# A decoder step's RWKV-7 state chain: the inverse folded into the reading matrix, and three engine orders rewritten

## The chip, the cores and the metric

The kernel runs on one core of a Trainium2 chip. The metric is the device time of one execution in microseconds (us).

## The reference

One step of a two-layer decoder over 512 prompt tokens and 8 sequences of 8 sampled tokens: a sliding-window attention layer, a SwiGLU layer, an RWKV-7 time mixing layer, and another SwiGLU layer, each with its normalisation. The change lies wholly in the RWKV-7 recurrence, for each of 16 heads of width 64:

```
sa = einsum('bhvk,bhk->bhv', S, -kk_t)
S  = S * d_t + sa * (kk_t * a_t) + v_t * k_t
o  = einsum('bhvk,bhk->bhv', S, r_t)
```

## The kernel before

**Stages.** Attention, the first SwiGLU layer and the projections r, k, v run until 868 us of the profile. The recurrence runs from there to 1248 us, the output projection and the second SwiGLU layer to the end. The time outside the recurrence is large products (line 779), which the change does not touch.

**The recurrence in chunks.** The 512 tokens are cut into 8 chunks of 64 (`NCH`, `CH`). Two heads, a pair, fill the 128 partitions. In a chunk the dependence of each token on the earlier ones is a triangular system. Its inverse `tt` is built without the state, and only then does the state `S_c` pass through the 8 chunks of the pair. For each chunk the state chain has four hops:

- TensorE `chain_u` (1178): u = (masked key-z product) v + z S_c, then VectorE `chain_u` (2458) copies it to `uc`;
- TensorE `chain_sa` (1193): tt times uc, then ScalarE `chain_sa` (1866) copies it to `sac`;
- TensorE `chain_s` (1204) adds b times sac to the state's bank, and VectorE `chain_s` (2463) scales it and writes `S_c`. ScalarE `scaled_state` (1861) prepares `spc` for that.

**Units and slots.** Unit 0 is the sampled tokens of all pairs, units 1 to 8 are the pairs of the prompt. The program is a software pipeline of 11 slots, s = 1 to 11, each with 8 steps c = 0 to 7. In slot s the engines prepare unit i = s (decays, keys; flag A1), build the inverse and the products of unit a = s-1 (A2), update the sampled state of pair j = s-2 (SB), run the state chain of pair q = s-3 (B), and normalise and gate pair g = s-4 (C). Slots 4 to 8 have all of it; slot 9 lacks A1, slot 10 has only B and C, slot 11 only C. Every engine has its own in-order list of this, written by hand (lines 1343 to 1424 for TensorE, 1931 to 2001 for ScalarE, 2543 to 2617 for VectorE). An engine that waits holds up all that stands behind in its list. ScalarE's `kk_root`, `gn_root`, `key_mix`, `merge_y`, `inverse_blocks`, VectorE's `masked_gram` and `hat`, and TensorE's `gram_*`, `level_*`, `merge_*`, `variance`, `bonus`, `gate` are such items. A `gram_` product goes to a bank of PSUM, and `masked_gram` reads it out.

**The transposed tokens.** The chain needs v, b and k of a unit with tokens on the partitions. VectorE transposes 32 by 32 blocks (`turned`, 2407) into a staging buffer, and SyncE moves the blocks to `tok` with 8 DMAs for each (`turned_in`, 548 to 554). There are two staging buffers: v and k share `reset`, b has `cc_s`. So k can't be transposed before v's copies have landed. In before that transpose stands at the end of step c = 2, ahead of the chain's copy of step 3.

**SyncE's queue in slot s** (569 to 582) is, in order: the 8 copies each of v, b and k; the store of a finished state `pw`; then a wait for the sampled state `sout`, which ScalarE writes as the last item of the slot; its store (580); and 8 loads of the sampled state of the slot after next (`state_in`, 541). The v copies of the next slot stand behind these. `sout` itself follows TensorE's `sample_update` (1265).

Of the kernel before, what the change touches and what calls it, by code (L numbers as in the profile page):

```python
# [22 lines left out]
P = 128  # L23
D = 1024
# [120 lines left out]
def build_program(nc, ins, outs, scratch):  # L145
    cols, width = constant_layout()
    ctx = ExitStack()
    with ctx:
# [14 lines left out]
        def const(name):  # L163
# [21 lines left out]
         tok_s, uc, sac) = region(  # L185
# [5 lines left out]
            ("gr", [P, 2, 3, SEQ], F32), ("tt", [P, 2, NCH, CH], F32), ("zr", [P, 3, NCH, 2, CH], F32), ("oS", [P, 2, SEQ], F32),  # L191
            ("g2h", [P, D], F32R), ("g2l", [P, D], F32R), ("g2m", [3 * G_REST, D], F32R), ("tok_s", [P, 3, SEQ], F32), ("uc", [P, 2, HD], F32),
# [83 lines left out]
        def tt_of(i):  # L276
            return tt[:, (i - 1) % 2] if i else tt_s
# [139 lines left out]
        def _(sp):  # L417
# [126 lines left out]
            def turned_in(i, which, name):  # L544

                sp.wait_ge(ev("turned_" + name), i + 1)
                if i >= 3:
# [214 lines left out]
        def _(pe):  # L762
# [284 lines left out]
            def lora2(i):  # L1047
# [4 lines left out]
                if i >= 2:  # L1052
                    pe.wait_ge(ev("kr"), i - 1)
                    pe.wait_ge(ev("kz"), i - 1)
                if i:
# [20 lines left out]
            def diag_gram(i):  # L1076
# [5 lines left out]
                if i >= 2:  # L1082
                    pe.wait_ge(ev("tt12"), i - 1)
# [61 lines left out]
            def gram_kz(i):  # L1145

                pe.wait_ge(ev("sig_a"), min(i + 2, UNITS))
                if i >= 3:
                    pe.wait_ge(ev("z"), i - 2)
                for c in range(NCH):  # L1150
                    for part in heads2:
                        out = mm(ps[part, G2, tk(c)], column(kx, i, part, c), zr_of(i)[part, c, 0, :], start=True, stop=True)
                out.then_inc(ev("kz_mm"), 1)

# [8 lines left out]
            def chain_ready(q):  # L1163

                for name in ("kz", "tt"):
                    pe.wait_ge(ev(name), q + 2)
                for name in ("tok_b", "tok_k", "tok_v"):
                    pe.wait_ge(ev(name), TURNED * (q + 2))
                pe.wait_ge(ev("tt12"), q + 1)
# [8 lines left out]
            def chain_u(q, c):  # L1178

                o = ps[:, CU, 0:HD]  # L1180
                if c == 0:
                    for part in heads2:
                        out = mm(o[part], gr[part, q % 2, 2, tk(0)], tok[part, q % 2, 2, tk(0)], start=True, stop=True)
                else:
                    pe.wait_ge(ev("sup"), NCH * q + c)
                    for part in heads2:
                        out = mm(o[part], zr[part, q % 3, c, 0, :], S_c[part, c - 1, :], start=False, stop=True)
                out.then_inc(ev("u"), 1)
# [101 lines left out]
            def variance(g):  # L1290
# [3 lines left out]
                pe.wait_ge(ev("kz"), min(g + 3, UNITS))  # L1294
# [36 lines left out]
            def gate_s(j):  # L1331

                at = slice(j * P, (j + 1) * P)
                mm(ps[:, IV, tk(j)], g2h[:, at], sgh[:, 0, SEQ:T], start=True, stop=False)
# [8 lines left out]
            def slot(s):  # L1343
# [9 lines left out]
                for c in range(NCH):  # L1353
                    if B:
                        chain_u(q, c)
# [7 lines left out]
                    elif c == 2 and C:  # L1363
                        centred(g)
                    elif c == 3:
                        if A2:
                            level_x(a, 2)
                        if CSM:
                            variance_s()
                    elif c == 4 and C:  # L1370
                        variance(g)
                    elif c == 5:
                        if whole:
                            level_y(a, 4)
                        if SB:
                            sample_read(j)
                        if CSM:
                            bonus_s()
                    elif c == 7 and whole:
                        merge_t(a)  # L1380
                    if B:
                        chain_sa(q, c)
                    if c == 2 and A2:
                        level_y(a, 2)
                    elif c == 4 and whole:
                        level_x(a, 3)
                    elif c == 5 and C:
                        bonus(g)
                    elif c == 6:
                        if SB:  # L1390
                            sample_sa(j)
                        if whole:
                            merge_y(a)
                        if C:
                            gate(g)
                    elif c == 7:
                        if A2:
                            gram_kz(a)
                        if SB:
                            sample_update(j)  # L1400
# [4 lines left out]
                    if c == 0 and A1:  # L1405
                        lora2(i)
                    elif c == 1 and A2:
                        level_x(a, 1)
                    elif c == 2 and A1:
                        kk_sum(i)  # L1410
                    elif c == 3 and whole:
                        level_y(a, 3)
                    elif c == 5:
                        if whole:
                            level_x(a, 4)
                        if SB:
                            sample_u(j)
                    elif c == 6:
                        if SB:
                            sample_out(j)  # L1420
                        if A2:
                            gram_br(a)
                    elif c == 7 and A2:
                        gram_kr(a)
# [21 lines left out]
        def _(act):  # L1446
# [419 lines left out]
            def chain_sa(q, c):  # L1866
# [4 lines left out]
                A(sac[:, c % 2, :], ps[:, CU, HD:P], ACT.Copy).then_inc(ev("sac"), 1)  # L1871
# [59 lines left out]
            for s in range(1, SLOTS):  # L1931
# [11 lines left out]
                for c in range(NCH):  # L1943
                    if B and c >= 1:
                        scaled_state(q, c)
                    if c == 0 and whole:
                        corner(a)
                    elif c == 1 and A2:
                        level_y(a, 1)
                    elif c == 2:  # L1950
                        if C:
                            dev_squares(g)
                        if CSM:
                            dev_squares_s()
                    elif c == 3 and A1:
                        kk_root(i)
                    elif c == 5 and whole:
                        level_y(a, 4)
                    elif c == 6:
                        if A1:  # L1960
                            key_mix(i)
                        if s == SLOTS - 1:
                            for b in range(2):
                                split_high(PH["ro"], b, b)
                    elif c == 7:
                        if whole:
                            merge_t(a)
                    if B:
                        chain_sa(q, c)
# [686 lines left out]
```

## Time and profile before

| | us |
|---|---|
| runs | 1768.16, 1763.10, 1766.89; median 1766.89 |
| profiled execution, its own time | 1760.71 |
| its span | 1758.9 |
| TensorE matmul busy | 1617.8 |
| VectorE busy | 889.4 |
| ScalarE busy | 629.3 |
| mean granted TensorE clock | 0.953 of full |

The span is the time from the first to the last instruction of the profiled execution. All times below count from the start of the span.

### The profile page before, as it was taken

The numbers are of one execution on the slowest core, as the hardware profiler recorded it, in microseconds if no ns is written. First come the engines' busy times: TensorE is split into PE (matmuls) and PEld (weight loads), VectorE is DVE, ScalarE is ACT, GpSimd is POOL, SyncE is SP. The second block draws the span as 40 slices with busy tenths as digits, with TensorE's granted clock in tenths as the row PEclk, the third lists the DMA queues.
The fourth block names the chain that finished last, engine by engine and source line by source line (L and its number), as shares of the span: only waits on it lengthen the run. The fifth ranks groups of instructions, "written<-read, shape, count | busy, mean of one in ns | idle before, by whom it ended". The sixth has DMA issues, their size and how long they took to land.

```text
span 1758.9 us, 44459 instructions
## 1 busy us (share of the span) xinstructions
PE 1617.8 (92%) x19218; PEld 1498.2 (85%) x19218; DVE 889.4 (51%) x1225; ACT 629.3 (36%) x1051; POOL 613.4 (35%) x322
## 2 busy tenths in 40 slices
PE   6989999999999977999878888888999999999995
PEld 6976999999999976888856666666799999999994
DVE  2156776666543237623354555543476666553233
ACT  3266333323221124333444455533343323322113
POOL 3335434434443321223332232310334444443430
PEclk9999999999999997999968999989799999999997
DMA  6610232222232223222222222210422222223221
GB/s 200 184 34 25 77 123 74 82 83 83 80 98 83 82 64 94 102 61 73 63 34 41 36 39 37 38 33 16 132 79 75 81 83 84 83 79 97 83 66 54
DMA packets 306018, 133.59 MB, mean 76 GB/s; under 512 B 119035, under 2 KB 302892, under 8 KB 305716
## 3 DMA queue, kind: packets, MB, share of 16 engines
q1 hardware_dynamic: 300850, 121.80, 25.7%
q10 hardware_dynamic: 5026, 9.70, 1.5%
q8 instruction: 112, 1.84, 0.4%
q14 instruction: 30, 0.25, 0.0%
HBM read 116.86 MB, written 12.64 MB: 74 GB/s over the span
## 4 chain that ended last, share of the span: by engine, by line
PE 77%; DVE 8%; issue 5%; SPq 5%; ACT 3%; DMA 1%; POOL 1%; ACTq 0%; DVEq 0%; POOLq 0%
PE ps L779 63%; SPq L554 3%; SPq L541 2%; DMA tok<-reset 1%; POOL wl L612 1%; ACT S L1654 1%; PE ps L1107 1%; PE ps L1197 1%; PE ps L1297 1%; PE ps L1027 1%; DVE xl_all L2070 1%; DVE mf L2327 1%; PE ps L1117 1%; PE ps L1302 1%; PE ps L1233 1%
## 5 line engine op out<-in xcount | busy, mean ns | idle before, releaser
L612 POOL TENSOR_TENSOR wl<-raw,wh 128x1024 fp32r<-128x1024 f32 (+1 forms) x172 | 479.8, 2790 | 780.1 <-ACT wh L1455 780.1
L779 PE MATMUL ps<-xh_all,wh 128*128 128x290 f32 (+1 forms) x2112 | 462.4, 300 | 29.0 <-DVE xl_all L2146 14.3
L779 PE MATMUL ps<-xh_all,wl 128*128 128x290 f32 (+1 forms) x2112 | 457.1, 298 | 0.0
L779 PE MATMUL ps<-xl_all,wh 128*128 128x290 f32 (+1 forms) x2112 | 456.3, 297 | 0.0
L1455 ACT CAST wh<-raw 128x1024 fp32r<-128x1024 f32 (+1 forms) x172 | 191.0, 1112 | 589.9 <-PE ps L779 581.5
L779 PEld LDWEIGHTS ps<-xh_all,wh 128*128 128x128 f32 x2112 | 344.0, 191 | 39.9 <-issue 15.9
L779 PEld LDWEIGHTS ps<-xl_all,wh 128*128 128x128 f32 x2112 | 343.3, 191 | 0.0
L779 PEld LDWEIGHTS ps<-xh_all,wl 128*128 128x128 f32 x2112 | 342.6, 191 | 0.0
L779 PE MATMUL ps<-hh,wh 128*128 128x288 f32 x704 | 148.1, 292 | 0.0
L779 PE MATMUL ps<-hl,wh 128*128 128x288 f32 x704 | 148.1, 292 | 0.0
L779 PE MATMUL ps<-hh,wl 128*128 128x288 f32 x704 | 148.1, 292 | 0.0
L2039 DVE TENSOR_TENSOR x<-x,ps 128x576 f32 (+1 forms) x32 | 24.1, 754 | 217.6 <-PE ps L779 211.1
L2183 DVE SCALAR_TENSOR_TENSOR lnw<-lnw,up_sc 128x576 f32<-128x576 f32 x44 | 122.2, 2777 | 1.5
L779 PEld LDWEIGHTS ps<-hh,wh 128*128 128x128 f32 x704 | 112.0, 187 | 0.0
L779 PEld LDWEIGHTS ps<-hl,wh 128*128 128x128 f32 x704 | 111.9, 187 | 0.0
L779 PEld LDWEIGHTS ps<-hh,wl 128*128 128x128 f32 x704 | 111.9, 187 | 0.0
L2048 DVE TENSOR_TENSOR lnw<-lnw 128x576 f32<-128x576 f32 x32 | 90.8, 2837 | 4.1 <-ACT lnw L1482 3.3
L2177 DVE COPY up_sc<-ps 128x2 f32<-128x2 f32 x44 | 7.0, 159 | 159.1 <-PE ps L779 159.1
L1575 ACT ACTIVATE hh<-lnw 128x576 fp32r<-128x576 f32 x44 | 30.1, 685 | 148.1 <-DVE lnw L2183 148.1
L706 POOL TENSOR_TENSOR zl<-oS,zh 128x512 fp32r<-128x512 f32 x8 | 10.1, 1268 | 172.0 <-ACT zh L1916 172.0
L2174 DVE SCALAR_TENSOR_TENSOR lnw<-lnr,gate_sc,lnw 128x576 f32<-128x576 f32 x44 | 58.5, 1329 | 4.7
L1573 ACT ACTIVATE lnw<-lnw,gate_sc 128x576 f32<-128x576 f32 x44 | 34.2, 777 | 69.3 <-DVE lnw L2174 69.3
(364 smaller groups left out, 2212.5 us busy)
## 6 DMA issues: line engine op xcount, KB each, us to landing
raw<-in_ffn_w_gu SPq DMA_DIRECT2D x88, 512.0 KB, 3.7
raw<-in_ffn_w_down SPq DMA_DIRECT2D x32, 704.0 KB, 4.4
raw<-in_rwkv_w_rkv SPq DMA_DIRECT2D x24, 512.0 KB, 3.7
raw<-in_attn_w_qkv SPq DMA_DIRECT2D x24, 256.0 KB, 3.5
raw<-in_attn_w_o SPq DMA_DIRECT2D x32, 128.0 KB, 2.9
tok<-reset SPq DMA_DIRECT2D x128, 32.0 KB, 2.4
raw<-in_rwkv_w_o SPq DMA_DIRECT2D x8, 512.0 KB, 3.7
spread<-table ACTq DMA_DIRECT2D x1, 3072.0 KB, 14.9
```

The costliest lines, as they stand in the source:

```text
L541: sp.dma_start(nat[block_rows(h, e), j % 2].rearrange("p b (f k) -> p b f k", f=2)[:, :, f], own[e][:, :, f]).then_inc(ev(f"nat_in{j % 2}" ...
L554: sp.dma_start(dst[block_rows(h, f), :, e], src[block_rows(h, e), :, f]).then_inc(ev("tok_" + name), 16)
L612: nc.gpsimd.tensor_tensor(wl[:, s, 0:ph.kb, :], raw[:, s, 0:ph.kb, :], wh[:, s, 0:ph.kb, :].bitcast(F32), ALU.subtract).then_inc(raw_free, 1)
L779: out = mm(ps[:, 2 * a + b, 0:n], w[:, s, k, :], o[:, k, b, 0:n] if wide else o[:, k0 + k, t0:t0 + TH], start=(first and k == 0 and w is w ...
L1027: out = mm(ps[part, bank + b, 0:TH], g1s[:, k, cols], mf[:, k % 2, t0:t0 + TH], start=(k == 0), stop=(k == KB - 1))
L1455: nc.scalar.copy(wh[:, s, 0:ph.kb, :], raw[:, s, 0:ph.kb, :]).then_inc(hi_done, 1)
L1573: A(gbuf[:, q, :], gbuf[:, q, :], ACT.Silu, bias=gate_sc[:, q, 1:2]).then_inc(ev("gated"), 1)
L1575: A(hh[:, bass.ds(2 * i + q, 1), :], hbuf[:, q:q + 1, :], ACT.Copy).then_inc(hid_hi, 1)
L2039: V.tensor_tensor(blk, blk, acc(a), ALU.add).then_inc(acc_free, 1)
L2048: V.tensor_tensor(squares, squares, lnw[:, 3:4, :], ALU.add).then_inc(ev("ln_acc"), 1)
L2174: V.scalar_tensor_tensor(g, centre, gate_sc[:, q, 0:1], g, ALU.mult, ALU.add).then_inc(ev("ffn_step"), 1)
L2183: V.scalar_tensor_tensor(h, h, up_sc[:, 1:2], g, ALU.add, ALU.mult).then_inc(up_free, 1)
```

## The change

The inverse is multiplied into the matrices that read the state, once for each unit, so that the chain loses the hop through `uc`: `chain_u` now yields sa itself. TensorE gets two new groups of 16 matmuls for each of units 1 to 8, `fold_read` (the masked product times the inverse) and `fold_seen` (z times the inverse). ScalarE copies each out of the bank (`folded_read`, `folded_seen`). For `fold_seen`, z is needed in transposed form as well, so VectorE has a fourth transpose, through the buffer `cc_s` that b uses, and SyncE 8 more copies, between b's and k's. `tt` has one buffer instead of two. The key-z product of units 1 to 8 is taken in the other orientation, and its mask is applied by one instruction with two operations.

The orders are rewritten. "Ahead" is between the chain's first and second product of a step, "behind" is after the second:

| step | TensorE ahead | TensorE behind | VectorE before its chain item | VectorE after it |
|---|---|---|---|---|
| 0 | diag_gram | lora2, centred | v transpose, sample_state | level_first |
| 1 | level_y 1 | level_x 1 | b transpose | level_x 1 |
| 2 | sample_read, level_y 2 | level_x 2 | cumulated | level_x 2 |
| 3 | kk_sum, level_y 3, sample_u | level_x 3 | sample_ut | kk_floor, level_x 3 |
| 4 | gram_kz, level_y 4, sample_sa | level_x 4 | sample_u, z transpose | level_x 4, unit_keys |
| 5 | variance, merge_y | merge_t | kz mask | k transpose, scaled_z |
| 6 | gram_br, bonus, sample_out | fold_read, gram_kr | hat, br mask | bonus, scaled_b |
| 7 | gate | fold_seen, sample_update | kr mask | sample_out, gated, mixed_keys, bonus_terms |

ScalarE's list has, after the chain's copy: step 3 level_y, kk_root, dev_squares; step 4 level_y, sample_sa, chunk_decays; step 5 merge_y, inverse_blocks, gn_root; step 6 folded_read, key_mix (and merge_t ahead of the chain's copy, behind scaled_state); step 7 folded_seen, operand_high, sample_update.

The diff, cut to what is not in the table:

```diff
-            return reset[:, PADP:PADP + SEQ] if which != 0 else cc_s[:, 0:SEQ]
+            return reset[:, PADP:PADP + SEQ] if which in (1, 2) else cc_s[:, 0:SEQ]
...
+        def turned_b_at(i):
+
+            return 2 * i if i else 1
+
+        def turned_z_at(i):
+
+            return 2 * i + 1
...
-                dst = tok_of(i)[:, which, :].rearrange("p (c e n) -> p c e n", e=2, n=HB)
+                dst = (ztok[:] if which == 3 else tok_of(i)[:, which, :]).rearrange("p (c e n) -> p c e n", e=2, n=HB)
...
-                    for which, name in ((2, "v"), (0, "b"), (1, "k")):
-                        turned_in(s - 1, which, name)
+                    turned_in(s - 1, 2, "v", s)
+                    turned_in(s - 1, 0, "b", turned_b_at(s - 1))
+                    if s >= 2:
+                        turned_in(s - 1, 3, "b", turned_z_at(s - 1))
+                    turned_in(s - 1, 1, "k", s)
...
+            def fold_read(i):
+
+                pe.wait_ge(ev("tt"), i + 1)
+                pe.wait_ge(ev("tt12"), i)
+                pe.wait_ge(ev("kz"), i + 1)
+                for c in range(NCH):
+                    for part in heads2:
+                        out = mm(ps[part, IV, tk(c)], gr_of(i)[part, 2, tk(c)], tt_of(i)[part, c, :], start=True, stop=True)
+                out.then_inc(ev("folded_mm"), 1)
+
+            def fold_seen(i):
+
+                pe.wait_ge(ev("folded"), read_at(i))
+                pe.wait_ge(ev("tok_b"), TURNED * turned_z_at(i))
+                for c in range(NCH):
+                    for part in heads2:
+                        out = mm(ps[part, IV, tk(c)], ztok[part, tk(c)], tt_of(i)[part, c, :], start=True, stop=True)
+                out.then_inc(ev("folded_mm"), 1)
...
-                out.then_inc(ev("u"), 1)
+                out.then_inc(ev("sa"), 1)
...
-            def chain_sa(q, c):
-
-                pe.wait_ge(ev("uc"), NCH * q + c + 1)
-                for part in heads2:
-                    out = mm(ps[part, CU, HD:P], tt[part, q % 2, c, :], uc[part, c % 2, :], start=True, stop=True)
-                out.then_inc(ev("sa"), 1)
...
-                pe.wait_ge(ev("kz"), min(g + 3, UNITS))
+                pe.wait_ge(ev("kz"), min(g + 4, UNITS))
...
+            def folded_read(i):
+
+                act.wait_ge(ev("folded_mm"), read_at(i))
+                A(gr_of(i)[:, 2, :], psb(IV), ACT.Copy, scale=-1.0).then_inc(ev("folded"), 1)
+
+            def folded_seen(i):
+
+                act.wait_ge(ev("folded_mm"), seen_at(i))
+                A(zr_of(i)[:, :, 0, :], chunks(psb(IV)), ACT.Copy).then_inc(ev("folded"), 1)
...
+                if which == 3:
+                    out, src = chunks(out), zr_of(i)[:, :, 0, :]
...
-            def chain_u(q, c):
-
-                dve.wait_ge(ev("u"), NCH * q + c + 1)
-                V.tensor_copy(uc[:, c % 2, :], ps[:, CU, 0:HD]).then_inc(ev("uc"), 1)
...
+                    elif c == 1 and A2:
+                        turned(a, 0, "b", "tok_b", 2 * a - 1 if a else 0)
...
+                        if whole:
+                            turned(a, 3, "b", "tok_b", turned_b_at(a))
...
+                        if A2:
+                            turned(a, 1, "k", "tok_v", a + 1)
```

## Rows read from the trace of the kernel before

**Rows 1.** Timeline of the SyncE queue: start, length, line, DMA, count.
```profile
885.00 5.59 SPq L554 DMA_DIRECT2D tok_s<-reset  x8
...
923.98 1.37 SPq L580 DMA_DIRECT2D out_sw<-sout  x2
...
963.91 1.33 SPq L580 DMA_DIRECT2D out_sw<-sout  x2
...
1045.01 1.31 SPq L580 DMA_DIRECT2D out_sw<-sout  x2
1046.37 5.64 SPq L541 DMA_DIRECT2D nat<-in_state_wkv  x8
...
1058.84 6.32 SPq L554 DMA_DIRECT2D tok<-cc_s  x8
1065.26 5.52 SPq L554 DMA_DIRECT2D tok<-reset  x8
...
1166.67 1.31 SPq L580 DMA_DIRECT2D out_sw<-sout  x2
...
1205.74 1.63 SPq L580 DMA_DIRECT2D out_sw<-sout  x2
```

**Rows 2.** Chain of waits in slots 5 and 6: start, length, who held it.
```profile
1024.53 1.99 PE ps L1297 x2
...
1031.37 1.07 PE ps L1302 x2
...
1038.39 0.96 PE ps L1142 x32
...
1041.63 0.86 PE ps L1274 x4
...
1043.35 0.95 PE ps L1279 x32
...
1058.13 3.74 DMA tok<-reset
```

**Rows 3.** The tile cc_s: its copies issued by SyncE, and their landing.
```profile
L554 SPq DMA_DIRECT2D tok<-cc_s x64: 585/611/1768, 899.9 to 1183.7; - x64
...
DMA to landing us min/median/max: 1.9/2.0/3.8
```

**Rows 4.** VectorE timeline of slot 6; in brackets the idle time before.
```profile
1061.89 0.71 DVE L2424 STREAM_TRANSPOSE reset<-kx 128x512 f32<-128x512 f32 x1 [3.69 <-DMA tok<-reset]
...
1069.98 0.74 DVE L2492 SCALAR_TENSOR_TENSOR oS<-ps,prm,rsd 128x512 f32<-128x512 f32 x1
...
1075.40 0.41 DVE L2449 TENSOR_TENSOR xt<-xt,ps 128x256 f32<-128x256 f32 x1
```

**Rows 5.** TensorE timeline of slot 6.
```profile
1062.76 0.48 PE L1197 MATMUL ps<-uc,tt 64*64 64x64 f32 x4 [4.00 <-DVE uc L2461]
...
1066.24 1.65 PE L1297 MATMUL ps<-rsd,cst 128*128 128x512 f32 x2
```

**Rows 6.** Costliest groups by line, over the whole span.
```profile
L1197 PE MATMUL ps<-uc,tt 64*64 64x64 f32 x256 | 22.6, 255 | 17.7 <-DVE uc L2461 16.9
...
L2461 DVE COPY uc<-ps 128x64 f32<-128x64 f32 x64 | 13.3, 208 | 8.8 <-PE ps L1187 8.7
```

**Rows 7.** ScalarE timeline of slot 6.
```profile
1069.03 0.63 ACT L1911 ACTIVATE rsd<-rsd 128x512 f32<-128x512 f32 x1
...
1077.69 0.76 ACT L1840 ACTIVATE yb<-ps 32x256 f32<-32x256 f32 x2 [0.40 <-PE ps L1125]
...
1082.34 1.68 ACT L1858 ACTIVATE tt<-xt 32x256 f32<-32x256 f32 x4
```

**Rows 8.** TensorE timeline of slot 10.
```profile
1206.27 0.28 PE L1183 MATMUL ps<-tok,gr 64*64 64x64 f32 x4
...
1235.81 0.48 PE L1175 MATMUL ps<-cst,S_c 64*64 64x64 f32 x4
```

**Rows 9.** VectorE timeline of slot 2: the v transpose.
```profile
892.46 0.67 DVE L2424 STREAM_TRANSPOSE reset<-vv 128x512 f32<-128x512 f32 x1
```

More of the change, by code:

```diff
@@ L1354, in slot @@
                     if B:
[L1355 removed]
+                        chain_sa(q, c)
                     if c == 0 and A2:
@@ L1362, in slot @@
                             centred_s()
-                    elif c == 2 and C:
-                        centred(g)
-                    elif c == 3:
-                        if A2:
-                            level_x(a, 2)
+                    elif c == 2:
+                        if SB:
+                            sample_read(j)
+                        if A2:
+                            level_y(a, 2)
+                    elif c == 3:
+                        if A1:
+                            kk_sum(i)
+                        if whole:
+                            level_y(a, 3)
+                        if SB:
+                            sample_u(j)
                         if CSM:
                             variance_s()
-                    elif c == 4 and C:
-                        variance(g)
-                    elif c == 5:
+                    elif c == 4:
+                        if A2:
+                            gram_kz(a)
                         if whole:
@@ L1375, in slot @@
                         if SB:
-                            sample_read(j)
+                            sample_sa(j)
+                    elif c == 5:
+                        if C:
+                            variance(g)
+                        if whole:
+                            merge_y(a)
                         if CSM:
                             bonus_s()
[L1379 to L1388, printed above, removed]
                     elif c == 6:
+                        if A2:
+                            gram_br(a)
+                        if C:
+                            bonus(g)
                         if SB:
[L1391 to L1400, printed above, removed]
+                            sample_out(j)
+                    elif c == 7 and C:
+                        gate(g)
                     if CSM:
@@ L1404, in slot @@
                         chain_s(q, c)
-                    if c == 0 and A1:
-                        lora2(i)
+                    if c == 0:
+                        if A1:
+                            lora2(i)
+                        if C:
+                            centred(g)
                     elif c == 1 and A2:
                         level_x(a, 1)
-                    elif c == 2 and A1:
-                        kk_sum(i)
+                    elif c == 2 and A2:
+                        level_x(a, 2)
                     elif c == 3 and whole:
-                        level_y(a, 3)
-                    elif c == 5:
-                        if whole:
-                            level_x(a, 4)
-                        if SB:
[L1417 to L1424, printed above, removed]
+                        level_x(a, 3)
+                    elif c == 4 and whole:
+                        level_x(a, 4)
+                    elif c == 5 and whole:
+                        merge_t(a)
+                    elif c == 6:
+                        if whole:
+                            fold_read(a)
+                        if A2:
+                            gram_kr(a)
+                    elif c == 7:
+                        if whole:
+                            fold_seen(a)
+                        if SB:
+                            sample_update(j)
             for s in range(1, SLOTS):
@@ L1945, in _ @@
                         scaled_state(q, c)
+                    if c == 6 and whole:
+                        merge_t(a)
+                    if c == 2 and CSM:
+                        dev_squares_s()
+                    if B:
+                        chain_sa(q, c)
                     if c == 0 and whole:
                         corner(a)
[L1948 to L1969, printed above, removed]
-                    if c == 1:
+                    elif c == 1:
+                        if A2:
+                            level_y(a, 1)
                         if A1:
@@ L2405, in bonus_terms, with turned @@
                 V.tensor_tensor(own, own, kx[:, :, SEQ:T], ALU.mult).then_inc(ev("f"), 1)
-            def turned(i, which, name, earlier, count):
+            def turned(i, which, name, free, count):
                 if count:
-                    dve.wait_ge(ev(earlier), TURNED * count)
+                    dve.wait_ge(ev(free), TURNED * count)
                 if which == 1:
```

186 lines of the change are left out of this document (109 added, 77 removed).

## The prediction

> **What bounds the kernel now.** Only the stage of the recurrence, 868 to 1248 us, changes, and in it the length of a slot is what counts. I took the SyncE queue's timeline first. The stores of the sampled state mark the slots: slot 3 ends at 963.91 and slot 8 at 1166.67 [rows 1], five slots of 40.55 us. Then I followed the chain of waits through one slot. In it the reader is to see a loop that runs through the queue. From the store of `sout` at 1045.01 SyncE issues two stores, eight loads (5.64 us from 1046.37), then the v copies, which end when b's begin at 1058.84 [rows 1]. The last v copy lands 3.74 us after its issue at 1058.13 [rows 2]. Only then can VectorE transpose k at 1061.89, after 3.69 us of idleness [rows 4]. The chain's next item stands behind it, so TensorE idles 4.00 us and comes back at the lower clock [rows 5]. From the store to the end of that transpose are 17.6 us; from there to the next `sout` some 23.6 us of steps 3 to 7.
>
> The hop that the change removes is on this path only in those steps. TensorE idle before the tt product and VectorE idle before the copy are 17.7 and 8.8 us in the whole stage [rows 6].
>
> **The parts of the change, and their cost.** I follow the same loop in the new order.
>
> *The hop.* 64 copies of 0.208 us go from VectorE, and 64 pairs of products with their wait from TensorE [rows 6]. On a bare chain a hop is 0.33 + 0.21 and the signals, some 0.6 us, 4.8 for each pair; in a full slot the long groups cover most.
>
> *The k transpose* goes from step 2 to step 5. In the rows v lands 16.9 us after the store (1061.87 less 1045.01) [rows 1, 2]; step 5 is later than that, so this wait is gone. What is late next is the z transpose in step 4. It uses `cc_s`, and must wait until b's copies of the same unit have landed. They are issued by 1058.84 + 6.32 = 1065.16, 20.15 us after the store [rows 1]. The last takes 0.61 and lands 2.0 after its start [rows 3], so at +21.5. With the transpose itself, about 0.7 like k's [rows 4], it ends at T = +22.3. When would VectorE have arrived? By adding up steps 0 to 3 in the table's order (diag_gram, lora2, centred and level 1 some 7 us, then steps of 3 to 3.7 us set by a level and the ScalarE work between) I get some 16 us after the slot's start. VectorE stands idle for about 6 us, longer than now.
>
> *Behind it* stand the chain item of step 4, level_x 4, unit_keys, and the kz mask, and TensorE's `variance` now waits for that mask. Times after T: chain item 0.3; level_x two instructions of 0.41 and about 0.45 [rows 4]; unit_keys 0.74, by the hat of the same shape and kind [rows 4]; mask 0.7. `variance` starts at 2.8, not at 1.2, and at the low clock takes 2.0 [rows 2], to 4.8. merge_y, the chain's second product, merge_t and the next first product take 2.9, to 7.7. ScalarE has merge_y's copies (0.76), inverse_blocks (1.68) and gn_root (0.68 + 0.63) one after another [rows 7], from 5.6 to 9.4. So `bonus` waits until 8.85 and ends at 9.9, and the second product of step 6, whose `sac` copy stands behind gn_root, scaled_state and merge_t's 0.76, starts at 10.85. After it fold_read and gram_kr, 0.96 each like gram_br [rows 2], to 13.4. Step 7: first product 0.55, gate 1.15, second product 0.6, fold_seen 0.96, sample_update 0.86 + 0.86 + 0.95 [rows 2], to 19.35. `sout` and its signals 0.65: 20.0.
>
> The loop is thus 22.3 + 20.0 = **42.3 us, against 40.55: 1.75 more in each of slots 4 to 8, +8.8.** Fewer hops in steps 5 to 7 don't show, because gram_br, gram_kr and the fold groups now stand there and in before some of the work of these steps lay in the wait's shadow.
>
> *The new copies of z* cost SyncE 8 x 0.61 and gaps, by b's row 6.3 [rows 1]. They end at T + 6.3 and land by T + 7.8, ahead of fold_seen at T + 15.7; k's end at T + 12.6 and land at T + 14.5, ahead of the next slot at T + 19.4. The queue, with `pw`, is free at T + 13.9, before `sout`. They cost nothing while that cover of 5 us stands; the floor they set is 22.3 + 13.9 = 36.2 us a slot. *The two ScalarE copies* (0.6 each) and the strided z transpose: covered in steps 6 and 7 by gate and by sample_update; without the cover 1.2 a slot. *The mask in one instruction*: 0.74 for 0.69, nothing.
>
> *Slots 1 and 2.* The v transpose of slot 2 now stands ahead of level_first and waits for slot 1's k copies. Their issue ends at 885.00 + 5.59 = 890.59 [rows 1], landing at about 892.4; in before the transpose ran at 892.46, behind level_first [rows 9]. So level_first starts at 893.8, not 890.3: +3.5. The fold groups at the low clock and a shorter end of slot 1 roughly cancel: +4.
>
> *Slot 3* has no normalisation: without variance, bonus, gate and gn_root its end is 4 us shorter, 38.2 against 963.91 - 923.98 = 39.9 [rows 1]: -1.7. *Slot 9*: no state loads stand before its v copies, so b lands some 5.7 us earlier and the wait nearly closes: 34 against 1205.74 - 1166.67 = 39.1: -5. *Slot 10* is the bare chain with some groups, 29.5 us from 1206.27 to 1235.81 [rows 8]. Adding up the new order with 2.4 to 3.2 us a step, and 5 in step 5 where bonus_s stands before the chain item, gives 24.5: -5. Slot 11 is the same.
>
> Sum: +4 - 1.7 + 8.8 - 5 - 5 = **+1.1 us**. The profiled execution took 1760.71 and would take 1761.8; it lies 6.2 below the median of the runs, and I give the time on the median's footing, 1766.9 + 1.1 = **1768 us**.
>
> **Bounds.** The end of the loop, 20.0 us, is the one uncertain term, counted five times. Below: TensorE's own work after T, 14.5 us at the full clock (bonus 1.07, not 1.99 [rows 2]), with the start and `sout`, is 15.5, so 37.8 a slot, -13.8 in the five instead of +8.8. Above: all TensorE work from 4.8 to 13.4 at the low clock, +3 a slot. I take 20.0 because each of its waits has a named item in front. The landing of b is between 1.9 and 3.8 [rows 3]; I take the median.
>
> In slot 6 the clock is low when TensorE comes back from 4.00 us of idleness, and 3.5 us later variance still takes 1.65 instead of 1.06 [rows 5]. TensorE: Matmul & The Clock Gate in the Trainium skill (Part 1, what you observe) has it that after an idle stretch the engine runs at half rate until it has been kept busy; by this the longer wait speaks against the change, which the row agrees with, and the time would be that of the second rival.
>
> **Rivals.**
>
> *The waits inside the end of the loop are shorter than I make them* (faster). If the kz mask, gn_root and merge_t fall into gaps, the slot goes halfway to the bound, 40.0, so 2.3 less in each of five: 1756 to 1757; at the full bound 1745. For it: TensorE's list has in each step one long group, so something usually is there to do. Against: `variance` waits for a mask four VectorE instructions behind T, and that can't be hidden.
>
> *The clock stays low* (slower). Place: steps 5 and 6 of slots 4 to 8. The idle time before is 6 us, not 4, and then TensorE has 0.8 us of work and waits again for the mask. If the low level holds through step 6, +3 a slot, +15 in all: 1783. It decides as soon as the low level lasts over 5 us after T; half of it gives 1775. For it: the low clock in slots 5 and 6. Against: from variance on the engine is busy.
>
> *The z transpose finds b landed* (faster), when steps 0 to 3 take over 21 us or the copies are issued sooner: then a slot is TensorE's work and its short waits, 35 us, for slots 3 to 8 -32, with the others 1729. DMA: Bandwidth & Descriptors (rules for kernel authors) advises to issue a DMA early and wait on its semaphore late, since the fixed cost then overlaps; moving the k wait from step 2 to 5 follows that, and by this rule alone the slot would lose its wait. The rows speak against it: the queue, not the landing, makes b late, by 20.15 of the 21.5 us.
>
> *The fold doesn't take the hop off the path* because it was covered: that is in the forecast for slots 4 to 8, and only slot 10 tells.
>
> **How the numbers follow.** About 0.3% (5.3 us) is what a measurement of this kernel can tell from no change. The forecast, with half a microsecond a slot either way, 0.36, lies within. The low clock 0.32, slower. Shorter waits 0.26 and the z transpose free 0.06, faster: 0.32. The range leaves out the last and the extreme of the two others: 1749 to 1784.
>
> **What would show it.** Of the changed kernel: the chain of waits goes store, loads, v, b, landing of a `cc_s` copy, z transpose, in slots 4 to 8; VectorE idles some 6 us before it; k's transpose waits for nothing; the stores of `sout` are 42 us apart in slots 4 to 8 and 34 in slot 9; slot 10 takes 25 us; TensorE waits 1.6 us for the kz mask before variance; the granted clock of the stage is lower. I am wrong if the z transpose is not the longest wait, if the slots are under 40 us or over 44, or if slot 2 is no longer than before.

## The result, and the profile after

The changed kernel takes 1788.9 us (median of 4 runs, 1783.99 to 1796.06) against 1764.99 (4 runs): a ratio of 1.0138, 95% interval 1.0097 to 1.0179. It is slower by 24 us. The forecast was 1768, the range 1749 to 1784, so the result lies outside it; the slots, too, lie over the 44 us at which the prediction called itself wrong. The profiled execution took 1790.78; its span is 1789.0. What lies behind the recurrence is unchanged (509.6 us, 510.8 before). The recurrence, from the first diagonal product to the first of the next projection, grew from 379.3 to 401.6 us. Another 9.0 of the 30.1 us between the two spans lie ahead of it in unchanged code; they are scatter: in the second run of the same kernel they were 3.6.

The SyncE queue of the changed kernel, where the stores of `sout` mark the slots, as in [rows 1]:

```profile
936.81 1.37 SPq L602 DMA_DIRECT2D out_sw<-sout  x2
977.03 1.32 SPq L602 DMA_DIRECT2D out_sw<-sout  x2
...
1067.15 1.31 SPq L602 DMA_DIRECT2D out_sw<-sout  x2
1068.51 6.08 SPq L557 DMA_DIRECT2D nat<-in_state_wkv  x8
1074.68 5.89 SPq L573 DMA_DIRECT2D tok<-reset  x8
1080.67 6.86 SPq L573 DMA_DIRECT2D tok<-cc_s  x8
...
1202.68 1.31 SPq L602 DMA_DIRECT2D out_sw<-sout  x2
1243.30 1.31 SPq L602 DMA_DIRECT2D out_sw<-sout  x2
```

From 977.03 to 1202.68 are five slots of 45.13 us, against 40.55. Part by part, from store to store, with the start of the first diagonal product and that of the next projection at the two ends:

| | before | after | difference | forecast |
|---|---|---|---|---|
| slots 1 and 2 | 55.2 | 59.0 | +3.8 | +4 |
| slot 3 | 39.9 | 40.2 | +0.3 | -1.7 |
| slots 4 to 8 | 202.8 | 225.6 | +22.9 | +8.8 |
| slot 9 | 39.1 | 40.6 | +1.5 | -5 |
| slots 10 and 11 | 42.3 | 36.1 | -6.2 | -5 |

VectorE of the changed kernel, transposes of z and of k in slots 4 to 7; in brackets the idle time before:

```profile
1001.17 0.71 DVE L2484 STREAM_TRANSPOSE cc_s<-zr 128x512 f32<-128x512 f32 x1 [3.67 <-DMA tok<-cc_s]
1008.05 0.70 DVE L2484 STREAM_TRANSPOSE reset<-kx 128x512 f32<-128x512 f32 x1
1044.52 0.71 DVE L2484 STREAM_TRANSPOSE cc_s<-zr 128x512 f32<-128x512 f32 x1 [1.82 <-DMA tok<-cc_s]
...
1088.91 0.71 DVE L2484 STREAM_TRANSPOSE cc_s<-zr 128x512 f32<-128x512 f32 x1 [1.11 <-DMA tok<-cc_s]
1099.15 0.70 DVE L2484 STREAM_TRANSPOSE reset<-kx 128x512 f32<-128x512 f32 x1
1135.57 0.71 DVE L2484 STREAM_TRANSPOSE cc_s<-zr 128x512 f32<-128x512 f32 x1 [0.28 <-DMA tok<-cc_s]
```

The k transpose, which in [rows 4] had stood idle for 3.69 us, waits for nothing. The z transpose waits for b's copies as forecast, but for 1.9 us a slot in the mean, not 6: VectorE comes to it some 20.5 us after the store, not 16. Why it is late, the timeline of TensorE in slot 6 shows:

```profile
1073.33 0.62 PE L1141 MATMUL ps<-xt,yb 32*32 32x32 f32 x49
1075.71 0.32 PE L1141 MATMUL ps<-xt,yb 32*32 32x32 f32 x15 [1.76 <-issue]
...
1078.18 0.47 PE L1247 MATMUL ps<-sac,tok 64*64 64x64 f32 x3
1079.72 0.26 PE L1247 MATMUL ps<-sac,tok 64*64 64x64 f32 x1 [1.06 <-issue]
...
1088.38 1.15 PE L1177 MATMUL ps<-kx,zr 64*64 64x64 f32 x32 [1.13 <-issue]
...
1092.08 0.66 PE L1141 MATMUL ps<-xt,yb 32*32 32x32 f32 x53 [0.91 <-issue]
...
1095.45 2.04 PE L1336 MATMUL ps<-rsd,cst 128*128 128x512 f32 x2 [2.22 <-DVE gr L2517]
...
1101.15 1.92 PE L1166 MATMUL ps<-zr,bt 64*64 64x64 f32 x32
1103.00 2.07 PE L1341 MATMUL ps<-rr,cst 128*128 128x512 f32 x2
```

Two things are to be seen. TensorE stops in the middle of groups of like products (after 49 of 64, after 3 of 4), where nothing is left to wait for; the view calls such time "issue", a wait that it can't attribute. And variance (L1336) waits 2.22 us for the kz mask and then runs at the low level of the clock, as do gram_br (L1166) and bonus (L1341); in [rows 2] the last took 1.07. In slots 4 to 8 gram_br takes 1.92 us every time and bonus 1.3 to 2.1, while variance is between 1.1 and 2.1, no slower than before (1.6 to 2.1). The waits of TensorE from 980 to 1210 us, about slots 4 to 8 (total, times, longest):

```profile
PE ps L1141 <- issue: 10.9, 8, 1.8
PE ps L1336 <- DVE gr L2517: 10.3, 5, 2.2
PE ps L1241 <- ACT pw L1938: 3.2, 5, 0.6
PE ps L1131 <- issue: 2.2, 2, 1.3
PE ps L1177 <- issue: 1.6, 2, 1.1
```

I call a stop any idle stretch of TensorE over 0.4 us between two products of one line. In the stage of the kernel before there are 8, together 6.9 us; after the change 26, together 29.2 us, nearly all in the groups of steps 1 to 4. The 22.3 us more equal what the stage lost; that alone proves nothing, since a stop can also take the place of another wait.

### The profile page after: what moved, and what is told of

Same layout as the page of the kernel before. It is cut to its first block, busy times and chain, and to the rows that moved or that the text cites. A ratio compares the mean times of both kernels' runs of the same rounds, so it can differ in the third digit from the quotient of the medians.

```text
span 1789.0 us, 45033 instructions
## 1 busy us (share of the span) xinstructions
PE 1636.4 (91%) x19474; PEld 1518.7 (85%) x19474; DVE 886.5 (50%) x1169; ACT 634.4 (35%) x1067; POOL 612.6 (34%) x322
## 4 chain that ended last, share of the span: by engine, by line
PE 82%; issue 6%; DVE 6%; ACT 3%; POOL 1%; SPq 1%; DMA 0%; ACTq 0%; DVEq 0%; POOLq 0%
PE ps L801 62%; PE ps L1141 2%; PE ps L1131 1%; ACT S L1699 1%; PE ps L1095 1%; PE ps L1247 1%; PE ps L1049 1%; POOL wl L634 1%; PE ps L1336 1%; PE ps L1166 1%; PE ps L1233 1%; SPq L573 1%; PE ps L1341 1%; DVE mf L2385 1%; DVE xl_all L2128 1%
## 5 line engine op out<-in xcount | busy, mean ns | idle before, releaser
L2097 DVE TENSOR_TENSOR x<-x,ps 128x576 f32 (+1 forms) x32 | 24.1, 753 | 219.9 <-PE ps L801 211.4
L2106 DVE TENSOR_TENSOR lnw<-lnw 128x576 f32<-128x576 f32 x32 | 86.6, 2707 | 4.0 <-ACT lnw L1527 3.2
L1620 ACT ACTIVATE hh<-lnw 128x576 fp32r<-128x576 f32 x44 | 30.1, 685 | 148.1 <-DVE lnw L2241 148.1
```

The costliest lines, as they stand in the source:

```text
L1620: A(hh[:, bass.ds(2 * i + q, 1), :], hbuf[:, q:q + 1, :], ACT.Copy).then_inc(hid_hi, 1)
L2097: V.tensor_tensor(blk, blk, acc(a), ALU.add).then_inc(acc_free, 1)
L2106: V.tensor_tensor(squares, squares, lnw[:, 3:4, :], ALU.add).then_inc(ev("ln_acc"), 1)
```

## The experiments

Each run stands beside the kernel before on the same chip. Where two experiments are compared by their times, they may come from different chips, on which the kernel before took 1762.4 to 1764.2 us. Where its name begins with a, it starts from the changed kernel, with b from the kernel before. The changed kernel once more:

> The changed kernel once more, beside the experiments, for its stage of the recurrence (first diagonal product to the first product of the output projection: 379.3 us before, 401.6 after) and for the 8 us that the profile of after was late before that stage began, in code that is the same in both. If those 8 us belong to the change, the stage begins at about 877 us again; if they are scatter of the start, it begins nearer 869. The stage itself should be within 2 us of 401.6.

It took 1789.4 us, ratio 1.0139 (1.0101 to 1.0178); its stage took 401.0 us, with 27 stops of 30.6 us, and its slots 4 to 8 44.7 us each. Two runs of one kernel thus differ by 0.4 us a slot.

**Is it the queue? z in a buffer of its own.**

```diff
-            return reset[:, PADP:PADP + SEQ] if which in (1, 2) else cc_s[:, 0:SEQ]
+            return zst[:] if which == 3 else reset[:, PADP:PADP + SEQ] if which in (1, 2) else cc_s[:, 0:SEQ]
```

> The changed kernel with z's transposed blocks staged in a buffer of their own (the memory of two tiles of the inverse that are idle by then), so that the z transpose no longer waits for b's copies. Queue theory (the loop through the SyncE queue and the z transpose sets the slot, as predicted): the 11.5 us of waits for b's copies go and the slots shorten by as much or more, stage 390 or less. TensorE theory (its gaps without instructions and its low clock set the slot, the wait for b is mostly a coincidence): the stage shortens by under 5 us.

It took 1786.4 us, ratio 1.011 (1.0061 to 1.0159). No wait of the z transpose is left, and slots 4 to 8 still take 45.2 us (stage 405.7). So the queue loop, on which the forecast stood, is not what holds a slot after the change.

**State loads ahead of the wait for `sout`**, in both kernels:

```diff
                 if 0 <= j < NPAIR:
+                    if j + 2 < NPAIR:
+                        state_in(j + 2)
                     sp.wait_ge(ev("sout"), j + 1)
...
-                    if j + 2 < NPAIR:
-                        state_in(j + 2)
```

> The changed kernel with SyncE's eight loads of the sampled state issued behind k's copies and ahead of the wait for sout, not behind it. b's and z's copies start some 5.7 us sooner after a slot's end. Queue theory: z's wait for b is gone, and the stage is 390 us or less. TensorE theory: under 5 us shorter; if the gaps in TensorE's stream come from the load of those copies, they move or go.

> The same move of the eight loads in the kernel before. There v's copies start 5.7 us sooner, so k's transpose in step 2 should find v landed. Queue theory: the 3.7 us wait and the low clock behind it go, 3 to 4 us for each of six slots, the whole time 15 to 25 us shorter. Rival: TensorE's own work and gaps take the place of the wait, under 8 us shorter.

The changed kernel took 1785.4 us (ratio 1.0125, 1.008 to 1.017), slots of 44.0, but the stage as a whole is no shorter (400.9 us). The kernel before took **1749.4 us, ratio 0.9915 (0.9877 to 0.9952), faster than both**; its slots 4 to 8 fell to 37.7 us and the granted clock in them rose from 0.92 to 0.98. The kernel before was bound by the queue, then, as [rows 1, 2] were read; the changed one is not.

**Half of the inverse's products** (the rest is left out, from slot 2 on), in both kernels with the early loads:

```diff
             def level_y(i, level):
...
-                for c in range(NCH):
+                for c in range(NCH // 2 if i else NCH):
```

and the same in `level_x`.

> The kernel after with the state loads ahead of the wait for sout, and in every slot from the second only 4 of the 8 chunks in the products of the inverse's levels (half of these products is left out; the copies behind them stay). It stands against the same kernel with all products, 1785.4 us. Instruction supply theory (TensorE runs through steps 1 to 4, where two levels stand in each step, faster than its instructions come, and stops at the boundaries of blocks of 256): the work itself saves up to 2.7 us a slot, and most of the 27 us of stops inside groups of like products go too: stops under 10 us, slots 4 to 8 5 us shorter than 44.3, time 1735 to 1745. Rival (the stops are nothing but slack, the slot is set by the work between TensorE, VectorE and ScalarE): at most the work saved, time 1760 to 1775, stops still about 20 us or turned into waits for copies.

> The kernel before with the state loads ahead of the wait for sout, and the same half of the inverse's products left out. It stands against the same kernel with all products, 1749.4 us, whose stops inside groups were only 4.4 us. Both theories: only the work saved, 2.7 us a slot where TensorE is the limit and less where a copy is, so 0 to 27 us; I expect 12: 1737. Under the supply theory it gains much less than the changed order gains by the same cut; under the rival both gain the same.

The changed order gained 49.9 us (1785.4 to 1735.5), the old one 16.7 (1749.4 to 1732.7); in slots 4 to 8 it is 6.5 us a slot (44.0 to 37.5) against nothing (37.7 to 37.8), and in the stage 53.4 us (400.9 to 347.5) against 12.6 (366.4 to 353.8). The profiled execution of the old order with half of the products was the slowest of four, 6.3 us above their median, and its clock in the slots was 0.92 for 0.98, so that "nothing" may be a little too low. Stops in the changed order fell from 23 of 27.4 us to 6 of 3.7. The same work left out is worth far more where two levels stand in each step.

**Are the stops tied to a count of instructions?** The first 32 products of the stage are done three times, twice and seventeen times (here three times), all on the changed kernel with the early loads:

```diff
-                for c in range(NCH):
+                for c in list(range(NCH)) * (1 if i else 3):
```

> The kernel after with the state loads ahead of the wait for sout, and the first 32 products of the stage done three times (same operands, same result), so that 128 more instructions of TensorE stand ahead of all that follows, half a block of 256. Supply theory: the stops stay at instructions 35 or 36 of every 256 counted from the first product of the stage, and so fall 128 instructions earlier in the work, in other groups of products than before (a stop of the kernel without it at level_x's line L1141 moves off it by half a block); their number and sum, 23 and 27 us, stay within a third. Rival (the stops belong to certain products or banks): they stay with the same products, and the remainder counted over 256 moves by 128. Time within 6 us of 1785 by either.

It could not tell. A product of this kernel is recorded as two weight loads and two products, so the 64 added ones were 256 instructions, not 128: a whole block, and all stops stayed where they were (26 stops of 32.3 us; 1790.1 us, one run). It gave something else, though, the first products of the stage in its TensorE timeline:

```profile
872.48 1.42 PE L1112 MATMUL ps<-zr_s,outs_s 64*32 64x32 f32 x145 [0.74 <-ACT vv L1759]
877.34 0.86 PE L1112 MATMUL ps<-zr_s,outs_s 64*32 64x32 f32 x47 [3.43 <-issue]
```

Nothing stands between them but 3.43 us of "issue". Half a block tells the theories apart:

> The kernel after with the state loads ahead of the wait for sout, and the first 32 products of the stage done twice (same operands, same result). Each is recorded as two weight loads and two products, so this adds 64 recorded products, 128 instructions: half a block. (Done three times they added a whole block, and the stops stayed where they were, as they had to by either theory.) Supply theory: the stops fall 64 recorded products earlier in the work. In slot 3 the kernel without it stopped before the last 10 products of sample_read, the last 26 of level_x, the last 46 of level_y and the last 2 of level_x; with it none of these four stops stays at that place, and each new one lies 64 products ahead of an old one or of the old block's boundary. Rival (the stops belong to certain products, buffers or banks): they stay at those places. Time within 6 us of 1785 by either.

The stops of slot 3 in the kernel without it (TensorE timeline):

```profile
939.53 0.46 PE L1272 MATMUL ps<-zr_s,s0t 64*64 64x16 f32 x10 [1.06 <-issue]
943.64 0.63 PE L1141 MATMUL ps<-xt,yb 32*32 32x32 f32 x26 [1.15 <-issue]
952.06 0.59 PE L1131 MATMUL ps<-xs,lm 32*32 32x32 f32 x46 [0.77 <-issue]
955.61 0.24 PE L1141 MATMUL ps<-xt,yb 32*32 32x32 f32 x2 [1.56 <-issue]
```

and with it:

```profile
942.58 0.64 PE L1141 MATMUL ps<-xt,yb 32*32 32x32 f32 x29 [2.33 <-issue]
946.88 0.42 PE L1131 MATMUL ps<-xs,lm 32*32 32x32 f32 x10 [0.30 <-issue]
955.64 0.21 PE L1141 MATMUL ps<-xt,yb 32*32 32x32 f32 x1 [1.27 <-issue]
959.22 0.33 PE L1260 MATMUL ps<-gr,tok 64*64 64x64 f32 x2 [0.53 <-issue]
```

None stayed in its place (1788.4 us, one run; 22 stops of 25.2 us in the stage, for 23 of 27.4). The first new one lies before the last 29 products of the level_x ahead of sample_read: 22 of sample_read's, 12 of the chain's and some 30 of level_x's, 64 products earlier than the old one. Counted from the first product of the stage (weight loads, products and TensorE's semaphore instructions), every stop over 0.5 us comes at instruction 35 or 36 of a block of 256, in this kernel 21 of 21, in the changed kernel 23 of 23, in the kernel before 7 of 7.

The trace holds the fetches too. Among the DMA queues (packets, MB, share) it lists two for instructions. This one has packets of 16,384 bytes; the line is that of the changed kernel, with and without the early loads:

```profile
q8 instruction: 114, 1.87, 0.5%
```

All 23 stops over 0.5 us of the changed kernel, and all 7 of the kernel before, end 1.2 to 1.6 us after such a packet has ended. TensorE goes on when the next block has come. And the rate:

> The kernel after with the state loads ahead of the wait for sout, and the first 32 products of the stage done seventeen times (same operands, same result): 1024 more instructions of TensorE, four blocks of 256 exactly, with no wait between them, so everything behind keeps its place in its block. Where they were done three times, 145 of them ran in 1.42 us, and then came a stop of 3.43 us. Supply theory: a stop at every boundary, each block takes 3 to 5 us though its products need some 1.3, the repeated products add 12 to 20 us, and this measures the rate at which instructions come. Rival (the stop there was a single event): the 512 added products run at their own rate, 5 to 7 us more in all.

```profile
875.62 1.93 PE L1112 MATMUL ps<-zr_s,outs_s 64*32 64x32 f32 x128 [3.15 <-issue]
879.35 1.93 PE L1112 MATMUL ps<-zr_s,outs_s 64*32 64x32 f32 x128 [1.80 <-issue]
883.35 1.93 PE L1112 MATMUL ps<-zr_s,outs_s 64*32 64x32 f32 x128 [2.07 <-issue]
...
898.26 1.93 PE L1112 MATMUL ps<-zr_s,outs_s 64*32 64x32 f32 x128 [1.80 <-issue]
901.72 0.86 PE L1112 MATMUL ps<-zr_s,outs_s 64*32 64x32 f32 x47 [1.53 <-issue]
```

Each stretch is 128 weight loads and 128 products, 256 instructions. They run in 1.93 us, and each stretch begins 3.73 us after the one before it in the mean (875.62 to 901.72 in seven; 3.5 to 4.0). The added work was eight blocks, not four, and the same queue has eight packets more:

```profile
q8 instruction: 122, 2.00, 0.5%
```

It lengthened slots 1 and 2 by 30.6 us, 3.8 a block, and the whole by 28.2 (1813.6 us, one run): the supply theory's rate holds, its sum was set too low by the same miscount. In this stretch each packet starts 1.0 to 1.4 us after the block before it has begun to run and takes 0.9 to 1.5, and the products go on 1.2 to 1.6 us after its end. So the 3.73 us look like one round trip for each block, not like a limit of bytes a second; no run varied that.

With 3.73 us a block I can set the chain's steps against their supply. Means of slots 4 to 8, each step from the chain's write of the state to the next, with the weight loads recorded in it (128 to a block); the other five steps go on to the same point of the next slot:

| | steps 2 to 4, us | weight loads | at 3.73 a block | the other five, us | clock, slots 4 to 8 |
|---|---|---|---|---|---|
| before | 16.6 | 424 | 12.4 | 23.8 | 0.92 |
| before, early loads | 13.7 | 424 | 12.4 | 24.1 | 0.98 |
| the same, half of the products | 14.0 | 264 | 7.7 | 23.7 | 0.92 |
| after | 17.4 | 568 | 16.6 | 27.7 | 0.83 |
| after, early loads | 16.0 | 545 | 15.9 | 28.0 | 0.86 |
| the same, half of the products | 11.6 | 375 | 10.9 | 26.2 | 0.90 |

In every form of the changed order steps 2 to 4 take what their instructions take to arrive, within 0.8 us. In the old order they take 1.3 us or more over it. The change hardly added instructions (46 packets in slots 4 to 8, 45 before); it packed them.

The table also shows what the supply does not explain. Of what a slot grew (4.6 us from store to store), steps 2 to 4 have only some 0.8 and the other five steps 3.9. The supply takes back what the removed wait should have given (17.4 us, where the old order without its wait takes 13.7); the loss against the kernel before lies mostly in the other steps, and the next experiments look for it there.

**Without the fold's work** (no z transposes and copies, no fold groups, no copies of them; the chain reads the unfolded matrices, so this part of the computation is left out):

```diff
-                        if whole:
-                            fold_read(a)
...
-                        if whole:
-                            fold_seen(a)
```

> The kernel after without the work of the fold: no transposes and copies of z, no two groups of 64 products and no two copies of them on ScalarE (their part of the computation is left out: the chain reads the unfolded matrices). What is left is the one-hop chain and the new order. Stages as in the kernel after: 401.6 us. If the fold's own work costs what its rows say on TensorE (two groups of 0.96 to 1.1 us) and half a block of instructions, slots shorten by 2.2 to 3 us: stage 378 to 382, time 1765 to 1769. If the fold's work lies in slack, as my forecast had it for the copies, it changes under 0.5 us a slot: over 1783. If the queue (z transpose behind b's copies) is what costs, then slots 4 to 8 fall to 40 us and the time to 1760 or less.

It took 1776.2 us, ratio 1.0068 (1.0035 to 1.01); slots 4 to 8 took 43.3, 1.8 less than in the changed kernel's first run and 1.4 less than in its second. The stage fell by 10.3, less than expected, since the slots at its end gained nothing. The fold itself is the smaller part of the loss; the order is slow without it.

**The k transpose alone**, moved to the end of step 5:

```diff
-                        if A2:
-                            turned(a, 1, "k", "tok_v", a + 1)
...
+                        if A2:
+                            turned(a, 1, "k", "tok_v", a + 1)
```

> The kernel before with the k transpose moved from step 2 to the end of step 5 of each slot, and nothing else: the part of the change that takes away VectorE's wait of 3.7 us for v's landing. It stands against 1764. Queue theory (the loop of before is closed by that wait): slots 4 to 8 shorten by 2 to 3 us, 366 to 370 us of stage as against 379.3, time 1750 to 1755, about what the earlier loads gave. Rival (what holds the slot is the sum of the work and its short waits): under 1 us a slot, over 1759.

> The kernel before with both: state loads ahead of the wait for sout, and the k transpose at the end of step 5. It stands against 1749.4 with the loads alone, where that transpose waits for nothing any more. Queue theory: the two remove the same wait, so they don't add: 1747 to 1751. If they add (each gave time by another way): 1740 or less.

Alone it gave nothing: 1765.3 us, ratio 1.0003 (0.9972 to 1.0034). With the early loads it took 1760.2, ratio 0.999 (0.997 to 1.0009), so that it lost 11 us of what these give (13 by the two ratios). The first miss is instructive. Its timeline in slot 6, VectorE and TensorE:

```profile
1074.80 0.67 DVE L2424 STREAM_TRANSPOSE reset<-kx 128x512 f32<-128x512 f32 x1
1075.39 0.19 DVE L2461 COPY uc<-ps 128x64 f32<-128x64 f32 x1
...
1075.63 0.33 PE L1197 MATMUL ps<-uc,tt 64*64 64x64 f32 x4 [1.06 <-DVE uc L2461]
...
1076.75 0.73 PE L1308 MATMUL ps<-sgh,g2h 128*128 128x512 f32 x1
```

The transpose now stands ahead of the chain's copy of step 6; TensorE idles 1.06 us, and gate, behind it, is slow (L1308 takes 723 ns in the mean, 498 in the kernel before; L1309 581 and 391). Steps 3 and 4 gained 2.6 us a slot, steps 6 and 7 lost 2.6. The wait was on the path, yet what this move gained was paid back three steps later.

**The wait for the kz mask**, in the changed kernel with the early loads:

```diff
                     elif c == 5:
-                        if C:
-                            variance(g)
                         if whole:
                             merge_y(a)
+                        if C:
+                            variance(g)
```

and on VectorE unit_keys goes from step 4 to step 5.

> The kernel after with the state loads ahead of the wait for sout, merge_y ahead of variance in TensorE's step 5, and unit_keys moved from step 4 to step 5 on VectorE, so that the kz mask comes sooner and TensorE has work in hand while it waits (12 us of idleness ahead of variance in the stage). It stands against 1785.4. If waits for the mask are a cost of their own: 1.5 to 2.5 us less in each of slots 4 to 8, time 1773 to 1778. Supply theory (steps 1 to 4 hold the slot, and what is gained in step 5 only brings the next blocks of instructions sooner): under 1 us a slot, 1780 to 1786.

It took 1775.0 us, ratio 1.0082 (1.0058 to 1.0105): 10.4 us less, slots of 41.8. The mask was a cost of its own, 2.3 us a slot. What TensorE waits for from 980 to 1210 us, here slots 4 to 8 and most of slot 9, is now:

```profile
PE ps L1141 <- issue: 11.5, 9, 2.0
PE ps L1131 <- issue: 3.8, 4, 1.3
PE ps L1241 <- ACT pw L1938: 3.2, 5, 0.6
PE ps L1149 <- DVE xs L2510: 3.0, 6, 0.7
```

The wait of L1336 is gone, the stops are all there (26, 27.1 us in the stage).

## Why the prediction was wrong

**The head of the loop (T = 22.3 us).** The z transpose ended 22.2 to 24.9 us after the store, 23.1 in the mean, so T was nearly right, by the wrong cause. The step of the path that failed is "steps 0 to 3 in the table's order (... then steps of 3 to 3.7 us set by a level and the ScalarE work between)". Steps 2 and 3 took 5.6 and 6.4 us, because between the chain's writes of these steps stand two groups of a level each, and sample_read in the first: with step 4 there are 568 weight loads, which arrive in 16.6 us, and the three steps took 17.4. I costed each group by its own duration (0.75 us for 64 products) and never counted instructions. With them right, VectorE's wait shrinks to 1.9 us, and taking it away altogether changes nothing. So the path that the forecast followed, through the queue and the landing of b, does not set the slot.

**The end of the loop (20.0 us)** measured 22.1 from the transpose's end to the store, 2.1 more in each slot; this is the term of the sum that was mis-sized. In time it is the larger miss: slots 4 to 8 lie 14.1 us over their forecast, 10.3 by the end and 3.8 by the head. Its waits were named rightly, the kz mask 2.1 us in the mean for my 1.6; but gram_br runs at the low level, 1.92 us for 1.10 in the same view of the kernel before, and so does bonus in two slots of five, 2.07 for 1.12, and for a part of its time in the others. That is the rival "the clock stays low". Its price of 3 us a slot is not borne out: gram_br and bonus gave 0.8 and 0.6 us a slot, and variance was 0.4 shorter than before. Its reason was not right either. I let it hang on a long idle stretch before the z transpose, and there is none; the granted clock of slots 4 to 8 is 0.83, with stops of 1 to 2 us spread over steps 1 to 4 and the wait for the mask. In each of these slots the level is low twice, the first time before the z transpose; in the kernel before it is low once. Where the stops went (half of the products) it was 0.90, where the mask's wait went 0.88.

**Slots 3 and 9.** Forecast -1.7 and -5, measured +0.3 and +1.5. No state loads stand in the queue ahead of slot 9's copies, so by the queue its time should have fallen to 34; it takes 40.6. Its z transpose waits for nothing, yet ends only 19.8 us after the store, and 20.8 us follow. Steps 2 to 4 take 16.6 us for 15.9 of supply. Slot 9 alone is 6.5 us of the miss, and the prediction gave no sum for its 34. **Slots 1 and 2** (+3.8 for +4) **and the bare chain at the end** (-6.2 for -5) were right: in slot 2 the v transpose waited 2.9 us for the copies of k, as said, and at the end the hop that the change removes shows. **The copies of z** were costed at nothing, and with the fold groups and the ScalarE copies left out as well a slot is 1.4 to 1.8 us shorter. How that divides between the copies and the groups was not tried.

**The trace before had it.** In the groups by line of the kernel before, over its recurrence, level_x stands as

```profile
L1117 PE MATMUL ps<-xt,yb 32*32 32x32 f32 x2176 | 30.3, 205 | 5.8 <-issue 4.2 <-ACT yb L1834 1.5
```

and after the change (L1141) as

```profile
L1141 PE MATMUL ps<-xt,yb 32*32 32x32 f32 x2176 | 32.5, 208 | 19.8 <-issue 17.5 <-ACT yb L1879 2.2
```

The prediction says nothing of the 4.2 us of "issue". The Trainium skill's Runtime: NRT & Kernel Launch (Instruction fetch mechanics) says that an engine's instructions are refilled in blocks of 16 KiB, 256 of them, and that crossing a boundary is "mostly hidden". The first half agrees: the stops come every 256, the packets are 16,384 bytes. The second doesn't here: 3.73 us against 1.93 of running, 14.6 ns for each instruction where the engine needs 7.5.

**What stays open.** How much of the five other steps' 4 us is the low clock and how much is work moved there (variance, bonus, the fold) was not separated; the wait for the mask is 2.3 us of it, and without the fold's work these steps take 1.0 less. Why the clock is granted as it is was not tried, nor what sets the time of a block's round trip.

## What to carry to other kernels

Count instructions by stretch, not only durations. A stretch of small products costs the larger of its busy time and its supply, here some 3.7 us for 256 instructions, and packing two such groups together next to long ones that leave supply idle loses what spreading them would have hidden. When a wait is taken off the path by moving its owner, look at what the owner now stands ahead of: the cheaper cure here was to issue loads that depend on nothing ahead of a wait, two lines moved, 0.9% faster.

## What the runs showed that I had not expected

- TensorE takes 256 instructions each 3.73 us when they run without waits, though they execute in 1.93 us; the stops lie at one place of every block and end 1.2 to 1.6 us after a packet of an instruction queue.

- The same edit (half of the inverse's products) is worth 6.5 us a slot in one order and next to nothing in the other.
- The early loads raised the granted clock of slots 4 to 8 from 0.92 to 0.98: of the 2.85 us a slot that they gave, part may be TensorE at the higher level; it was not separated from the wait.
